# Second mixer's front in a new order: decays and compression ahead of the fills, convolution on ScalarE and GpSimd, gate sums inside the loop, factors by transposes

## What is computed

```python
z = rms_norm(x, norm_mix) @ w_in
y_a = rg_lru_mixer(z[lru_x], z[lru_g], ...)       # 4-tap convolution, two gates, a scan
y_b = short_conv_mixer(z[sc_b], z[sc_c], z[sc_x], ...)
y_c = fox_mixer(z[q], z[k], z[v], z[f], ...)      # 4 heads, forgetting attention
y_d = nsa_mixer(z[q], six k/v pieces, gates, ...) # compressed, selected, window branches
x = x + concat(rms_norm of each) @ w_out
x = x + (silu(gate) * up) @ w_down

# rg_lru_mixer
xc = causal_dwconv(xr, conv_w) + conv_b           # 4 taps
r = sigmoid(xb @ w_gates[0] + b_gates[0]); i = sigmoid(xb @ w_gates[1] + b_gates[1])
log_a = (-8 * softplus(-lam)) * r
a = exp(log_a); b = sqrt(-expm1(2 * log_a)) * (i * xc)   # then the scan h = a*h + b
# fox_mixer
c = cumsum(log_sigmoid(f_logit + f_bias))         # scores: q.k * scale + c_q - c_k
# nsa_mixer
gates = sigmoid(g_logit + g_bias)
kc = rms_norm(compress(...)); vc = compress(...)  # 15 blocks of 32 tokens -> 128 hidden -> 64
```

## Time and profile before

| what | us |
|---|---|
| median of 3 runs | 764.47 (764.35 to 764.59) |
| profiled execution | 764.53 |
| its span | 762.7 |
| around the span | 1.8 |
| PE busy | 730.4 |
| DVE busy | 551.8 |
| ACT busy | 448.5 |
| POOL busy | 63.6 |

### The profile page before, as it was taken

One profiled execution on the slowest core, in us unless ns is written; L12 is line 12 of the kernel. 1 busy time (PEld: TensorE's weight loads), 2 busy tenths in 40 slices (PEclk: granted clock), 3 DMA queues, 4 the chain that ended last, 5 costly groups with the idle time before them and its releaser, 6 DMA issues.

```text
span 762.7 us, 14055 instructions
## 1 busy us (share of the span) xinstructions
PE 730.4 (96%) x5000; PEld 656.4 (86%) x5000; DVE 551.8 (72%) x1066; ACT 448.5 (59%) x855; POOL 63.6 (8%) x94
## 2 busy tenths in 40 slices
PE   2899999999999999999999999899899999999998
PEld 2799898899999899999999999587798888888886
DVE  4887349898797786666666778687876877777764
ACT  4667466665745755545554677588655655555552
POOL 8001011000347000000000003000000000000000
PEclk9999999999999999999999999799999999999999
DMA  9997898888799357666666648622154766666631
GB/s 289 352 277 243 188 198 258 275 276 263 226 323 262 109 180 221 181 176 198 186 183 174 161 112 232 196 84 87 55 166 137 227 196 184 176 198 193 176 110 55
DMA packets 187236, 148.37 MB, mean 195 GB/s; under 512 B 13680, under 2 KB 171314, under 8 KB 187176
## 3 DMA queue, kind: packets, MB, share of 16 engines
q1 hardware_dynamic: 183296, 143.61, 63.9%
q10 hardware_dynamic: 2232, 3.03, 2.1%
q0 software_dynamic: 1664, 1.15, 0.7%
HBM read 146.44 MB, written 1.36 MB: 194 GB/s over the span
## 4 chain that ended last, share of the span: by engine, by line
PE 85%; DVE 6%; ACT 4%; DMA 2%; issue 2%; POOL 0%; SPq 0%; ACTq 0%; DVEq 0%; POOLq 0%
PE ps L2290 21%; PE ps L1903 15%; PE ps L1904 14%; PE ps L1905 14%; PE ps L2292 11%; DMA raw<-in_w_ada 2%; PE ps L2267 1%; DVE arena L1276 1%; PE ps L1951 1%; PE ps L2158 1%; ACT w_hi L717 1%; PE ps L2180 1%; PE ps L2145 1%; DVE w_lo L1218 1%; PE ps L2144 1%
## 5 line engine op out<-in xcount | busy, mean ns | idle before, releaser
L1218 DVE TENSOR_TENSOR w_lo<-raw,w_hi 128x1024 fp32r<-128x1024 f32 (+3 forms) x223 | 270.1, 1232 | 68.9 <-ACT w_hi L717 67.5
L2290 PE MATMUL ps<-h,w_hi 128*128 128x512 f32 x672 | 239.2, 396 | 0.0
L717 ACT ACTIVATE w_hi<-raw 128x1024 fp32r<-128x1024 f32 (+3 forms) x223 | 226.3, 1038 | 21.0 <-PE ps L1905 6.1
L2292 PE MATMUL ps<-h,w_lo 128*128 128x256 f32 x672 | 189.4, 282 | 0.0
L2290 PEld LDWEIGHTS ps<-h,w_hi 128*128 128x128 f32 x672 | 126.3, 188 | 29.6
L1903 PE MATMUL ps<-h,w_hi 128*128 128x256 f32 (+1 forms) x440 | 126.7, 288 | 2.4 <-ACT arena L887 0.9
L2292 PEld LDWEIGHTS ps<-h,w_lo 128*128 128x128 f32 x672 | 126.2, 188 | 1.0
L1904 PE MATMUL ps<-h,w_hi 128*128 128x256 f32 (+1 forms) x440 | 123.4, 280 | 0.0
L1905 PE MATMUL ps<-h,w_lo 128*128 128x256 f32 (+1 forms) x440 | 123.3, 280 | 0.0
L1903 PEld LDWEIGHTS ps<-h,w_hi 128*128 128x128 f32 (+1 forms) x440 | 82.8, 188 | 6.8 <-issue 4.9
L1904 PEld LDWEIGHTS ps<-h,w_hi 128*128 128x128 f32 (+1 forms) x440 | 82.9, 188 | 0.0
(11 more groups left out here) (376 smaller groups left out, 1257.0 us busy)
## 6 DMA issues: line engine op xcount, KB each, us to landing
raw<-in_w_in SPq DMA_DIRECT2D x53, 512.0 KB, 5.6
raw<-in_w_down SPq DMA_DIRECT2D x44, 512.0 KB, 4.3
raw<-in_w_gate_up SPq DMA_DIRECT2D x44, 512.0 KB, 4.3
raw<-in_w_ada SPq DMA_DIRECT2D x32, 512.0 KB, 4.6
raw<-in_w_gate SPq DMA_DIRECT2D x22, 512.0 KB, 3.9
raw<-in_w_up SPq DMA_DIRECT2D x22, 512.0 KB, 5.1
raw<-in_w_ada SPq DMA_DIRECT2D x32, 256.0 KB, 5.9
raw<-in_w_o SPq DMA_DIRECT2D x8, 512.0 KB, 5.3
```

Of the source, the lines that this page charges most:

```text
L717: A(w_hi[:, m % HL, 0:w], raw[:, n % RAW, 0:w], ACT.Copy).then_inc(hi_done, 1)
L1218: V.tensor_tensor(w_lo[:, m % HL, 0:w], raw[:, n % RAW, 0:w], w_hi[:, m % HL, 0:w].bitcast(f32), sub).then_inc(lo_done, 1)
L2290: T.matmul(bank[:, :], hi, h2[:, k, :, :].rearrange("p a b -> p (a b)"), start=(k == 0), stop=False, skip_group_check=True)
L2292: ins = T.matmul(bank[:, 0:SEQ], lo, h_hi[:, k, :], start=False, stop=(k == KC - 1), skip_group_check=True)
```

## The change

- **Order of the front.** TensorE runs the decays (small transposes and four rows) and the compression straight behind the norm sums. The decay rows no longer wait for `qk_rms`: row 0 goes into the bank of fill 0 in place of ps0. Fill 1 follows, with the compression's turn in its middle, then head factors 0 to 3, the small products, factors 4 and 5, the first scores, factor 6, fill 2. Four factors use other banks than before (`FAC_IN`).
- **Compression weights** are loaded two places earlier in SyncE's order (behind fill 3 in place of fill 5).
- **LRU convolution.** ScalarE does the first tap with the bias (`first_tap`), GpSimd the other three as a multiply and an add each (six instructions for a half). VectorE's part is gone.
- **LRU gate sums** (four matmuls) go to step 0 of the loop, behind the scores of the second pair; the activations on them and the decay's tanh and exp go into ScalarE's step 0.
- **Sigmoids by tanh** with scale 0.5; the halves are made up for in constants, in one VectorE instruction on the branch gates, and in the LRU's product.
- **Splits.** VectorE's splits for fill 4 and fill 5 and ScalarE's for fill 5 move into or next to step 0. VectorE's key factor of the compression moves into step 0 too.
- **Latent sums.** GpSimd adds the squares first (six adds); TensorE has four matmuls in place of 16.
- **Factors by transposes.** `spread` uses two transposes in place of two matmuls, and `residual` 16 transposes in place of 16 matmuls.

```diff
-EARLY = 2
+EARLY = 3
 FILL_AT = {0: 3, 1: 4, 2: 5, 3: 6, 4: 7, 5: 8, 6: 9}
 ADA_FIRST, ADA_LAST = 2 * KC, 5 * KC
 ADA_JOB = [range(ADA_FIRST + 3 * c // 2, ADA_FIRST + 3 * (c + 1) // 2) for c in range(16)]
...
     for kv in range(2):
...
                             [(0, 8, P, 0, P, I["nsa_cmp_w1_2"][kv].rearrange("(k p) n -> p k n", p=P)
                               [:, 8 * half:8 * half + 8, :])]))
-    for c in FILL[EARLY:]:
+    for c in FILL[2:]:
         chunk("fill", w_in2, c)
     for k in Y_ROWS:
         panel("wout", [(0, 1, D, 0, D, cols(I["w_out_2"], 0, D, k, 1))])
@@ -547,6 +547,8 @@
                ("fq", 0, fqT[:, 0, :], "fox_q"), ("fq", 1, fqT[:, 1, :], "fox_q"),
...
 
@@ -1060,9 +1062,10 @@
...
+                if more:
+                    split.ahead(outputs[l])
                 await_out(act, l)
                 line(A(FILL_TO[q], lin(l), ACT.Copy), free_name(l))
             split.ahead(nth("tok", 2) - AHEAD)
@@ -1087,15 +1090,29 @@
             line(A(cf[:, 1, :], cf[:, 1, :], ACT.Ln, bias=ones[:, 0:1]), "f_log")
...
+
...
+                if c == 0:
+                    act.wait_ge(s("pool_part"), 3)
+                l = L["fill"][c]
+                act.wait_ge(s(free_name(l)), freed[l][1])
+                line(A(xc[:, c, :], lx[:, c, 0:SEQ], ACT.Identity, scale=vcol("lru_conv_w_2", c), bias=vcol("lru_conv_b_2", c)),
+                     "tap_ready")
+
+            fill(0, False)
+            first_tap(0)
             act.wait_ge(s("qk_ss"), 1)
             line(A(rinv, ps[0][:, 0:SEQ], ACT.Sqrt, scale=1.0 / HD, bias=eps_c), "qk_rms")
-            fill(1)
+            split.ahead(nth("fill", 0))
 
             act.wait_ge(cmp_used, 4)
             line(A(part, ps[7][:, 0:2 * P], ACT.Copy), "hid_ready")
             act.wait_ge(s("hid_sum"), 1)
             line(A(hid[:, :, 0:NCMP], hid_pre, ACT.Gelu_apprx_tanh), "hid_ready")
+            fill(1, False)
+            first_tap(1)
             act.wait_ge(s("cmp_mm"), 2)
             line(A(kcT[:, 0:NCMP], ps[7][:, 288:288 + NCMP], ACT.Copy))
             line(A(kcq[:, 0:NCMP], ps[7][:, 288:288 + NCMP], ACT.Square), "kc_sq")
@@ -1106,12 +1123,24 @@
...
-            line(A(gate2, gate2, ACT.Sigmoid), "gate2_ready")
-            for q in range(4):
-                l = L["lru"][q // 2]
-                act.wait_ge(s("lru_mm"), 2 * (q // 2) + 2)
-                line(A((ra, ia)[q // 2][:, q % 2, :], lin(l, SEQ, SEQ * (q % 2)), ACT.Sigmoid,
-                       bias=vcol("lru_b_gates_2", q)), "lru_sig")
+            line(A(gate2, gate2, ACT.Tanh, scale=0.5), "gate2_ready")
+
+            def lru_gates():
+
+                act.wait_ge(s("lru_c"), 1)
+                for q in range(4):
+                    l = L["lru"][q // 2]
+                    act.wait_ge(s("lru_mm"), 2 * (q // 2) + 2)
+                    line(A((ra, ia)[q // 2][:, q % 2, :], lin(l, SEQ, SEQ * (q % 2)), ACT.Tanh, scale=0.5,
+                           bias=vcol("lru_b_gates_2", q)), "lru_sig")
+
+            def lru_decay():
+
+                act.wait_ge(s("lru_sig"), 2)
+                for c in range(2):
+                    line(A(yT[:, c, :], ra[:, c, :], ACT.Tanh, scale=spt[7][:, c:c + 1], bias=spt[7][:, c:c + 1]), "lru_tanh")
+                for c in range(2):
+                    line(A(ra[:, c, :], ra[:, c, :], ACT.Exp, scale=spt[6][:, c:c + 1], bias=spt[6][:, c:c + 1]), "lru_a")
...
-            act.wait_ge(s("lru_sig"), 4)
-            act.wait_ge(s("lru_c"), 1)
...
-            fill(EARLY)
+            fill(2, False)
+            split.ahead(nth("fill", 1))
...
+                if x == 0:
+                    lru_gates()
...
+                if x == 0:
+                    lru_decay()
...
+                    line(A(yT[:, 0:2, :], yT[:, 0:2, :], ACT.Sqrt, scale=0.25), "lru_sqrt")
...
-            split.ahead(nth("fill", 0))
-
-            dve.wait_ge(s("qk_rms"), 1)
-            line(V.reciprocal(rinv, rinv), "qk_inv")
-            lru_conv(0)
-            split.ahead(nth("fill", 1))
-
             dve.wait_ge(s("decay_mm"), 1)
...
-                if h == 3:
...
+                row = DECAY[h][:, 0:SEQ]
...
-            lru_conv(1)
+            dve.wait_ge(s("qk_rms"), 1)
+            line(V.reciprocal(rinv, rinv), "qk_inv")
+            dve.wait_ge(s("cmp_mm"), 1)
+            line(V.tensor_reduce(out=hid_pre, in_=ps[7][:, 0:2 * P].rearrange("p (a j n) -> p a n j", a=2, j=4)
+                                 [:, :, 0:NCMP, :], axis=mybir.AxisListType.X, op=add), "hid_sum")
             for n, q in enumerate(FAC):
                 _, _, dst, gain = QK2[q]
...
-                line(stt(out=dst, in0=dst, scalar=vcol(gain), in1=ps[n % 4][:, 0:SEQ], op0=mult, op1=mult), "qk_ready")
...
+                line(stt(out=dst, in0=dst, scalar=vcol(gain), in1=FAC_IN[n][:, 0:SEQ], op0=mult, op1=mult), "qk_ready")
...
+            split.ahead(nth("fill", 0))
...
-            split.ahead(nth("fill", EARLY))
-            dve.wait_ge(s("gate2_ready"), 1)
...
+                if x == 0:
+                    split.ahead(nth("fill", 1))
+                    dve.wait_ge(s("gate2_ready"), 1)
+                    line(V.tensor_scalar(gate2, gate2, 0.5, 0.5, mult, add))
+                    dve.wait_ge(s("kc_rms"), 1)
+                    line(V.reciprocal(kcq[:, 0:NCMP], kcq[:, 0:NCMP]))
+                    line.settle()
+                    line(stt(out=kcT[:, 0:NCMP], in0=kcT[:, 0:NCMP], scalar=vcol("nsa_kc"), in1=kcq[:, 0:NCMP], op0=mult,
+                             op1=mult), "kc_ready")
...
-                    line(V.tensor_tensor(ia, ia, xc, mult), "lru_in")
+                    line(stt(out=ia, in0=ia, scalar=1.0, in1=xc, op0=add, op1=mult), "lru_in")
...
+            for n in range(1, KC):
+                c = LAT_ORDER[n]
+                if c == 6:
+                    continue
+                pool.wait_ge(s("lat_sq"), n + 1)
+                to = 6 if c == 7 else 0
+                line(G.tensor_tensor(sq[:, to, :], sq[:, to, :], sq[:, c, :], add), "pool_part" if n == KC - 1 else None)
+                line.settle()
...
+            def lru_conv(c):
+
+                pool.wait_ge(s("tap_ready"), c + 1)
+                pool.wait_ge(s("xb_ready"), 1)
+                for k in range(1, 4):
+                    tap = vcol("lru_conv_w_2", 2 * k + c).to_broadcast([P, SEQ])
+                    line(G.tensor_tensor(tot[:, :], lx[:, c, k:k + SEQ], tap, mult))
+                    line.settle()
+                    line(G.tensor_tensor(xc[:, c, :], xc[:, c, :], tot[:, :], add), "xc_ready" if k == 3 else None)
+                    line.settle()
+            lru_conv(0)
             pool.wait_ge(s("qk_ready"), 1)
             for a in (0, HD):
                 pool.dma_start(kskw_x[a:a + HD, :], kskw[HD - a:2 * HD - a, :]).then_inc(s("kskw_x_in"), 16)
+            lru_conv(1)
...
-                    ins = T.matmul(dst[:, t * P:(t + 1) * P], v[:, t:t + 1].to_broadcast([P, P]), ident[:, :],
-                                   start=True, stop=True)
+                    ins = T.transpose(dst[:, t * P:(t + 1) * P], v[:, t:t + 1].to_broadcast([P, P]), ident[:, :])
...
-            pe.wait_ge(s("lat_sq"), 8)
+            pe.wait_ge(s("pool_part"), 1)
...
-            for q, (c0, c1) in enumerate(((0, 6), (6, 8))):
+            for q, c in enumerate((0, 6)):
                 for t in range(TT):
-                    for c in range(c0, c1):
-                        ins = T.matmul(ps[7][:, 2 * q + t:2 * q + t + WIDE], sq[:, c, t * P:(t + 1) * P], ones[:, 0:WIDE],
-                                       start=(c == c0), stop=(c == c1 - 1))
+                    ins = T.matmul(ps[7][:, 2 * q + t:2 * q + t + WIDE], sq[:, c, t * P:(t + 1) * P], ones[:, 0:WIDE],
+                                   start=True, stop=True)
...
-            chunk_out(L["fill"][1], hx)
...
-            pe.wait_ge(s("qk_rms"), 1)
+            l = L["fill"][0]
+            pe.wait_ge(s(free_name(l)), freed[l][1])
...
-                line(T.matmul(ps[h][:, 0:SEQ], selb[own, :], cf[own, 2, :], start=True, stop=True), "decay_mm")
+                line(T.matmul(DECAY[h][:, 0:SEQ], selb[own, :], cf[own, 2, :], start=True, stop=True), "decay_mm")
...
+            def part_turn():
+
+                pe.wait_ge(s("hid_ready"), 1)
+                for kv in range(2):
+                    ins = T.transpose(ps[7][:, P * kv:P * kv + P], part[:, P * kv:P * kv + P], ident[:, :])
+                line(ins, "cmp_mm")
+            chunk_out(L["fill"][1], hx, middle=part_turn)
...
                 if n < 4:
                     pe.wait_ge(s("dec_ready"), n + 1)
+                elif n < 6:
+                    pe.wait_ge(s("qk_ready"), n - 1)
                 else:
-                    pe.wait_ge(s("qk_ready"), n - 3)
-                line(T.matmul(ps[n % 4][:, 0:SEQ], head_rows[own, r * P:(r + 1) * P], rinv[own, :], start=True, stop=True),
+                    pe.wait_ge(s("vc_ready"), 1)
```

(31 more changed lines are left out.)

63 lines of the change are left out of this document (18 added, 45 removed).

## The result

The changed kernel took **757.44 us** (median of four, 754.57 to 759.59) where the kernel before, beside it on the same chip, took 764.41: a ratio of **0.9914** [0.9897, 0.9931]. That is 7.0 us or 0.9% by the medians and 6.6 by the ratio: inside the range, but only about half of the forecast 13.3, and 6.2 us above the forecast time. The sign was right, the size was not.

What follows compares the result with a forecast made beforehand. TensorE, busy 730.4 of 762.7 us, was taken to bound the kernel, partly waiting at a fallen clock. Front 8.1, latent sums 2.0, spreads 1.4 and residual 1.8 make 13.3: 764.5 - 13.3 = 751.2 us, range 748.5 to 758.0.

Steps and rivals of the forecast that it cites:

- What bounds the kernel, and the new order: Whole kernel: TensorE bounds it; around the second mixer's front it hangs on others, and the reordered front removes that.
- costed at 0.83 each: Front: GpSimd's twelve convolution instructions take 0.83 us each, hidden behind ScalarE's step 0, costing nothing.
- That rival (10%): Front: GpSimd's convolution is late, TensorE waits for it, the front gains only 1.5 us, total 757.8; chance 10%.
- the slower one (4%): Front: GpSimd's convolution holds TensorE, which returns at the lower clock; slower than before, 768.2 us at 2.0 each; chance 4%.
- The front's 8.1 us: Second mixer's front: step 1's turn starts at 498.3 instead of 506.36, gaining 8.1 us.
- The clock: Front: TensorE keeps 0.12 us per 256-column instruction, so fill 2 ends at 489.1.
- the clock still falls: Front: TensorE runs at the lower clock from 485 to 498.5; front gains 2.9 us, total 756.4; chance 10%.
- ScalarE's step 0: Loop step 0: ScalarE's copies, splits, exponentials and gates take 7.9 us, to 497.4, setting step 1's turn at 498.3.
- A: Latent sums: 24 of TensorE's 32 instructions go, 2.7 us; part may be given back, so 2.0, between 1.0 and 2.7.
- B: Spreads: 32 instructions become 16 transposes at 0.11 us, gaining 1.4 us, between 0.8 and 1.8.
- C: Residual: 32 instructions become 16 transposes, gaining 1.8 us, between 0 and 1.8.
- The prediction's upper end (748.8): Whole kernel: ScalarE's step 0 is 1.3 us shorter and A to C at their upper ends, gaining 15.7 us.

Runs made afterwards that it cites:

- x1: Changed kernel with the sums of the latents, the spreads and the residual put back, so only the new front remains; 760.94 us against 762.75 before, ratio 0.9964.
- x6: Changed kernel with fill 2's eight steps taken apart and put around head factors 4 and 5; 754.16 us against 763.44 before, ratio 0.9882.
- x8: Changed kernel with fill 2's steps taken apart and ScalarE's gates ahead of step 0's splits; 753.16 us against 763.38 before, ratio 0.9867.
- the first set: First measurement of the changed kernel, unaltered, beside the kernel before; 757.44 us against 764.41, ratio 0.9914.
- after_third: Changed kernel measured again, unaltered, beside the kernel before; 755.14 us against 763.38, ratio 0.9889.
- after_fourth: Changed kernel measured again, unaltered, beside the kernel before on another chip; 754.57 us against 763.49, ratio 0.9883.

## Where the prediction was right and where it failed

**What bounds the kernel, and the new order.** Right. Compression, scores and gate sums came where the working had put them, up to 485: the compression 0.3 us early against it, the first scores 1.4 late, with factors 4 and 5 behind the wait of 0.8 us and already at the fallen clock.

**GpSimd.** Right that it is never waited for, with room: costed at 0.83 each with the 0.08 between, measured 0.61 and 0.73 and about 0.08 between, 0.75 on average. That rival (10%) and the slower one (4%) fall.

**The front's 8.1 us: the step that failed.** It was mis-sized: 2.2 us in the profile of the result, and 1.8 to 2.7 as a kernel of its own (x1). Two steps of its working were wrong, and the yardstick was in doubt.
- *The clock.* The working let fill 2 take 2.9 us and end at 489.1, that is 488.1 in a stretch that starts a us earlier; it ended at 493.4. The step that failed is the pace of 0.12 us per instruction from 483 on; the rows have 0.22. The text said that the clock would stay, because of "a dense chunk from 479.4 to 482.7 and almost no idle after". The chunk was there, and the clock fell between 483 and 484, behind a wait of 0.8 us and among factors of 4 rows. The rival "the clock still falls" (10%) is what happened: front 2.9 and 756.4 by it, 2.2 and 757.44 measured. Its own evidence, small products that wait from 484 to 486, was the better. Against x6, where the clock stays up, it cost 2.9 us of front in that profile and 1.5 to 1.6 in the three others.
- *ScalarE's step 0.* The working had the gates behind three splits and an exponential and summed to 7.9 us, but asked only when step 1's turn would be ready, and not who stands still meanwhile: fill 3 needs the bank that the gates free. By its own numbers the first two gates end at 489.5 + 0.4 + 3.1 + 0.9 + 0.9 = 494.8, and fill 3, gathers and scores behind them (4.9) make 499.7 and not 498.3, so 1.4 of the 8.1 were not there. x8 against x6 has 1.45 us of front for it, of which 0.6 are given back in step 1.
- *The yardstick.* 8.1 was taken against an execution of before that lost 6.8 us to the clock. Others lose 3.4, with a front 1.8 to 2.0 shorter. In those that gain was not to be had; how much of the median's shortfall it makes isn't shown.

With the first two amended the front is 24.7, where 23.1 was forecast (31.2 - 8.1); the last 1.6 are not taken apart.

**A, latent sums, 2.0.** As a part alone 2.7. In the changed kernel it is whole where the gates' loads land in time and gone where they don't, as in the first set's profile. There the first scores come 2.5 us early and the second pair's level with before. The prediction had this ("part of it may be given back where the key and value copies wait for splits") but not that the clock falls behind such a wait, so its lower end of 1.0 was too high: it is nothing in such an execution.

**B and C, 1.4 + 1.8.** 2.8 measured for 3.2. By the rule of the Trainium skill (TensorE: Matmul & The Clock Gate, "Part 4: PE-mode transpose", about 275 ns for one inside a kernel) the transposes would have lost 1.8 us, an estimate. The rows have 272 and 281 ns as the *length* of one, but only 0.11 us from one to the next (the residual's come in fours, each four holding the chain for 0.44 us), and it is that which counts: the length agrees, the reading as a price doesn't.

**Sum as it came.** In the profile of the result: front 2.2, A 0, B and C 3.0 (1.0 ahead of the front, 2.1 behind it), together 5.2, the difference of the spans (762.7 - 757.5). The two faster executions of the set, 754.6 and 755.5, have no profile; after_third and after_fourth, profiled at 756.10 and 755.24, start the front 2.0 and 2.8 us earlier (A is kept there, and executions differ anyway) and have it 1.2 to 1.3 us shorter (clock). The prediction's upper end (748.8) has a slip: 498.3 - 497.1 is 1.2, not 1.3.

## What to carry to other kernels

Here a stretch at the lower clock wasn't cured by moving dense work near it. Look for small products and waits left in the new order, and try pieces of a dense accumulation between them; idle products cost here what they saved. When one engine's stretch is shortened, follow the next engine up to the bank that it frees, amend both, and measure at a mark late enough to see what is given back. Before a gain is read off one profiled execution, ask how much of it is that execution's own clock: two profiles of the same kernel differed by 1.8 us in 30.

## What the runs showed of the hardware

- The same kernel loses a different amount to the clock from one execution to the next: over the front 3.4 or 6.8 us before, 3.4 or 5.1 changed. In the six profiles with products put into the waits of the changed front it lost nothing there; with idle products in before's front (x10) it lost 5.1.
- Behind the up projections TensorE's waits of 0.87 to 1.84 us were followed by no fall of the clock (16 profiles), those of 1.90, 2.44, 3.28 and 3.68 us by one each, which lost 1.6 to 3.3 us. The length of the wait isn't all that counts: in the front of the changed kernel the clock fell behind a wait of 0.80 us among small products (0.76 from 483 to 484 us, 0.50 after), and in x6 it stayed at 1.00 behind one of 2.39 us.
- GpSimd takes 0.61 us for a 128x256 product with one operand spread from a column, 0.73 for a plain add of that size, while VectorE works mostly out of PSUM; 0.74 for the latents' adds.
- Loads of 512 KB issued while eight loads of 192 KB in rows of 1 KB were under way landed 8.1 to 13.4 us after issue (medians of 19 profiles); with the eight cut to 16 KB each, 5.4 us (one profile).
